# A hybrid attention and gating layer on eight cores: where its attention pieces stand among the full matrix products, and a closing norm in halves

## The reference

```python
h = rmsnorm(x, norm_g)
proj = einsum('bsd,de->bse', h, w_in) + b_in                 # 1024 -> 2816
q, k, v, z_a, u_s, v_s, z_s = split(proj, ...)
# 8 query heads, 2 key/value heads, window of 128, a learned sink per head
attn = banded_sink_attention(q, k, v, sinks) * silu(z_a)
# 8 channel groups, a masked lower-triangular 128x128 matrix each, chunks of 128
sgu = gelu(u_s) * (W_s @ layernorm(gelu(v_s)) + b_s) * silu(z_s)
x = x + concat([attn, sgu]) @ w_out + b_out                  # 1024 -> 1024
out = rmsnorm(x, final_norm_g)
```

## Time and profile before

| | |
|---|---|
| median of 3 runs | 523.46 us (521.31 to 564.06) |
| time of the profiled execution | 525.54 us |
| its span on the slowest core (core 1) | 524.0 us |
| spans of the eight cores | 514.8 to 524.0 us |
| TensorE busy (matmuls) | 498.0 us, 95% of the span |
| ACT, DVE, POOL busy | 63%, 57%, 45% |

### The profile page before, as it was taken

The page is one execution under the profiler, slowest core; times in us unless marked ns, Lnnn a source line. Parts: engine busy times, 40 slices in busy tenths (PEclk is TensorE's granted clock), DMA queues, the critical chain, the costliest instruction groups (busy, mean ns, idle before and its releaser), DMA issues.

```text
span 524.0 us, 10243 instructions; the slowest of 8 cores (514.8 to 524.0 us)
## 1 busy us (share of the span) xinstructions
PE 498.0 (95%) x3443; PEld 238.4 (45%) x3443; DVE 297.7 (57%) x429; ACT 332.0 (63%) x551; POOL 233.3 (45%) x270
## 2 busy tenths in 40 slices
PE   6798889999999999999999999999999999999993
PEld 2356345444454445444454445444454444544441
DVE  3865876564545465454646544554655546666556
ACT  4335768747688386865868476874859467757332
POOL 2101678360546415481374614473254774545213
PEclk9599989999999999999999999999999999999998
DMA  8999994810329422490229613292226303231024
GB/s 241 327 338 335 312 243 67 201 43 1 121 104 228 113 72 90 127 275 2 81 81 230 173 41 118 90 225 92 82 81 177 65 2 117 86 120 41 2 81 201
DMA packets 43876, 71.12 MB, mean 136 GB/s; under 512 B 27536, under 2 KB 27536, under 8 KB 43824
## 3 DMA queue, kind: packets, MB, share of 16 engines
q1 hardware_dynamic: 42480, 68.17, 43.6%
q0 software_dynamic: 1200, 2.25, 2.7%
q10 hardware_dynamic: 144, 0.05, 0.0%
HBM read 49.48 MB, written 16.78 MB: 126 GB/s over the span
## 4 chain that ended last, share of the span: by engine, by line
PE 81%; POOL 5%; ACT 4%; DVE 4%; issue 3%; DMA 2%; POOLq 0%; SPq 0%; ACTq 0%; DVEq 0%
PE pp L533 41%; PE pp L794 19%; PE pp L597 8%; PE pp L721 3%; PE pp L558 3%; PE pp L730 2%; DMA xa<-x 2%; PE pp L678 1%; PE pp L582 1%; POOL xa L778 1%; POOL uT L649 1%; ACT zsT L543 1%; PE pp L643 1%; POOL st_lr L613 1%; ACT junk L470 1%
## 5 line engine op out<-in xcount | busy, mean ns | idle before, releaser
L533 PE MATMUL pp<-xT,w_fm 128*128 128x512 bf16 x1088 | 253.2, 389 | 3.3 <-ACT xT L524 1.3
L533 PEld LDWEIGHTS pp<-xT,w_fm 128*128 128x128 bf16 x1088 | 106.3, 100 | 136.4 <-issue 27.8
L794 PE MATMUL pp<-w_out_bf,mixT 128*128 128x512 bf16 x512 | 118.6, 380 | 0.0
L778 POOL TENSOR_TENSOR xe<-xe,bout_sb 128x1024 f32<-128x1024 f32 x28 | 65.9, 2353 | 20.8 <-DVE xe L808 11.8
L794 PEld LDWEIGHTS pp<-w_out_bf,mixT 128*128 128x128 bf16 x512 | 47.7, 98 | 58.7 <-issue 4.5
L756 POOL TENSOR_TENSOR mixT<-LR,zaT 128x512 bf16<-128x512 f32 x28 | 32.4, 1156 | 58.8 <-DVE LR L752 54.8
L740 ACT ACTIVATE LR<-pp,esink 128x128 f32<-128x128 f32 x128 | 36.5, 369 | 26.0 <-PE pp L730 15.7
L808 DVE SCALAR_TENSOR_TENSOR xe<-xe,st_fr,gf_sb 128x1024 f32<-128x1024 f32 x28 | 35.9, 1284 | 25.7 <-POOL st_fr L806 14.0
L597 PE MATMUL pp<-w_vs,xT 128*128 128x512 bf16 x224 | 49.8, 379 | 0.1
L799 DVE TENSOR_TENSOR xe<-pp,xe 128x512 f32<-128x512 f32 x56 | 38.4, 686 | 19.9 <-PE pp L794 19.5
L543 ACT ACTIVATE zaT<-pp,pack_a_sb 128x512 bf16<-128x512 f32 x32 | 22.0, 688 | 42.3 <-PE pp L533 42.3
(11 more groups left out here) (84 smaller groups left out, 586.7 us busy)
## 6 DMA issues: line engine op xcount, KB each, us to landing
xa<-x SPq DMA_DIRECT2D x32, 512.0 KB, 5.8
xe<-x SPq DMA_DIRECT2D x28, 512.0 KB, 4.1
out<-xe SPq DMA_DIRECT2D x28, 512.0 KB, 2.8
xe<-w_in SPq DMA_DIRECT2D x12, 512.0 KB, 12.1
mixT<-w_in SPq DMA_DIRECT2D x10, 512.0 KB, 14.3
w_out_bf<-w_out POOLq DMA_DIRECT2D x8, 256.0 KB, 11.9
out<-xa SPq DMA_DIRECT2D x4, 512.0 KB, 2.7
LR<-sgu_wT SPq DMA_DIRECT2D x1, 512.0 KB, 16.1
```

Of the source, the lines that this page charges most:

```text
L533: ins = e.matmul(bank(h), lhsT=w_fm[:, FM.index(cb), k, :], rhs=xT[:, xb, k, :], start=(k == 0), stop=(k == 7))
L778: fn = lambda e: e.tensor_tensor(out=r[:, s, :], in0=r[:, s, :], in1=bout[:], op=ALU.add)
L794: ins = e.matmul(bank(h), lhsT=mixT[:, mb, ec, tt * 128:(tt + 1) * 128], rhs=w_out[:, ec, hf * 512:(hf + 1) * 512], start=(ec == 0), stop= ...
```

## The change

Three things change. First, the planner's input gets an ordering rule: for each stage the full products of its Exp phase are collected (fill), and the S of tile j is held until a given number of them are placed, five per tile in stages 1 to 5, two per tile in stage 6 with its eight tiles, one per tile in stage 0. The pv of tile j-1 is held until the S of tile j is placed. Second, the closing norm of the last stage is rewritten (close_tile): the gain is multiplied in before the statistics are known, into another buffer, and the final scaling is ACT's. Third, for the very last tile the norm goes by halves of 512 values: two sums of squares, the two means joined by a small DVE operation, one half scaled by ACT and one by DVE, two stores of 256 KB on two queues. An unused bank class is dropped.

```diff
+SPREAD = (1, 5, 5, 5, 5, 5, 2)
...
+        fill = {st: [] for st in range(-1, NS)}
+        scores = {st: [] for st in range(NS)}
+        values = {st: [] for st in range(NS)}
...
-            G.op("pe", mm, reads=xkeys(st, range(4)) + [("w", cb)], cost=1.73, alloc=[h], prio=prio, mode="full", gate=ph)
+            o = G.op("pe", mm, reads=xkeys(st, range(4)) + [("w", cb)], cost=1.73, alloc=[h], prio=prio, mode="full", gate=ph)
+            if func is None:
+                fill[st - 1].append(o)
...
+            scores[st - 1 if last else st].append(o)
...
+            values[st - 1 if last else st].append(o)
...
+        def close_tile(n, v0):
+            s = n % 4
+            end = n == NT - 1
+            z, zk = (vs_f[:, 0:2, :].rearrange("p a b -> p (a b)"), [("vs_f", 0), ("vs_f", 1)]) if end else (xe[:, s, :], [("xe", s, 0), ("xe", s, 1)])
+            parts = ((0, 512), (512, 1024)) if end else ((0, 1024),)
+            for i, (a, b) in enumerate(parts):
...
+                G.op("act", lambda e, a=a, b=b, i=i: e.activation(out=junk[:, a:b], in_=xa[:, s, a:b], func=AF.Square, accum_out=st_fe[:, s, i:i + 1]),
...
+                G.op("dve", lambda e, a=a, b=b: e.tensor_tensor(out=z[:, a:b], in0=xa[:, s, a:b], in1=gf[:, a:b], op=ALU.mult),
...
+            G.op("pool", lambda e: e.tensor_scalar(out=st_fm[:, s:s + 1], in0=st_fe[:, s, 0:1], scalar1=1.0 / D, scalar2=EPS,
+                                                   op0=ALU.mult, op1=ALU.add), reads=[("fe", s, 0)], writes=[("fm", s)], cost=0.19, prio=v0)
+            if end:
+                G.op("dve", lambda e: e.scalar_tensor_tensor(out=st_fm[:, s:s + 1], in0=st_fe[:, s, 1:2], scalar=1.0 / D, in1=st_fm[:, s:s + 1],
...
+            G.op("pool", lambda e: e.tensor_tensor(out=st_fr[:, s:s + 1], in0=st_fm[:, s:s + 1], in1=nh[:, 0:1], op=ALU.pow),
...
+                if i == 0:
+                    G.op("act", lambda e, a=a, b=b: e.activation(out=xa[:, s, a:b], in_=z[:, a:b], func=AF.Copy, scale=st_fr[:, s:s + 1]),
...
+                else:
+                    G.op("dve", lambda e, a=a, b=b: e.tensor_scalar(out=xa[:, s, a:b], in0=z[:, a:b], scalar1=st_fr[:, s:s + 1], scalar2=None, op0=ALU.mult),
...
+                G.op(("sp", "act")[end and i == 0], lambda e, a=a, b=b: e.dma_start(out=out_d[n * 128:(n + 1) * 128, a:b], in_=xa[:, s, a:b]),
...
+        for st in range(NS - 1):
+            between = sorted(fill[st], key=lambda o: (o.prio, o.n))
+            for j, o in enumerate(scores[st][1:], 1):
+                o.after += (between[SPREAD[st] * j - 1],)
+                values[st][j - 1].after += (o,)
```

More of the change, by code:

```diff
@@ L109 @@
     ENGS = ("pe", "act", "dve", "pool", "sp")
[L110 to L111 removed]
+    CAPS = {"S": 4, "V": 2, "P": 4}
+    PLACES = {"S": (0,), "V": (4, 6), "P": (6, 7, 5, 4)}
     def __init__(self, graph, warm, warmed):
@@ L560, in mmv @@
                 return ins
-            G.op("pe", mmv, reads=xkeys(st, range(4)) + [("w", CB_V)], cost=1.79, alloc=[h], prio=v0 + 0.3, mode="full")
+            o = G.op("pe", mmv, reads=xkeys(st, range(4)) + [("w", CB_V)], cost=1.79, alloc=[h], prio=v0 + 0.3, mode="full")
+            fill[st - 1].append(o)
             def vsrc(lo, a, b):
@@ L599, in mmvs @@
                     return ins
-                G.op("pe", mmvs, reads=[("xT", xb, tt)] + [("w", CB_VS + c) for c in range(4)], cost=1.73,
+                o = G.op("pe", mmvs, reads=[("xT", xb, tt)] + [("w", CB_VS + c) for c in range(4)], cost=1.73,
                      alloc=[h], prio=v0, mode="full", gate=3 * st - 1)
+                fill[st - 1].append(o)
             G.op("dve", lambda e: e.tensor_tensor(out=vs_f[:, vb, :], in0=bank(h), in1=bvs[:], op=ALU.add), uses=[h],
@@ L687, in mms @@
                 return ins
-            G.op("pe", mms, reads=[("qT", qb, c) for c in range(4)] + [("kT", (n - 1) // 4 % 3), ("kT", n // 4 % 3)], cost=0.45, alloc=[S],
+            o = G.op("pe", mms, reads=[("qT", qb, c) for c in range(4)] + [("kT", (n - 1) // 4 % 3), ("kT", n // 4 % 3)], cost=0.45, alloc=[S],
                  prio=v0 - 10, mode="quad", gate=ph)
+            scores[st - 1 if last else st].append(o)
             if first:
@@ L779, in load_xe @@
             G.op({"pool": (2.35, fn)}, None, reads=["c_bout"], writes=keys, prio=st + 0.4 + 0.1 * s, port=True)
+        def close_tile(n, v0):
[4 more added lines that the diff above has]
+            for i, (a, b) in enumerate(parts):
+                ykeys = [("xh", s, i)] if end else [("xh", s, 0), ("xh", s, 1)]
+                zkeys = [zk[i]] if end else zk
+                G.op("act", lambda e, a=a, b=b, i=i: e.activation(out=junk[:, a:b], in_=xa[:, s, a:b], func=AF.Square, accum_out=st_fe[:, s, i:i + 1]),
+                     reads=ykeys, writes=[("junk", "junk1")[i], ("fe", s, i)], cost=0.38 + 0.87 * (b - a) / 1024, prio=v0 - 0.7)
+                G.op("dve", lambda e, a=a, b=b: e.tensor_tensor(out=z[:, a:b], in0=xa[:, s, a:b], in1=gf[:, a:b], op=ALU.mult),
+                     reads=ykeys + ["c_gf"], writes=zkeys, cost=0.04 + 1.24 * (b - a) / 1024, prio=v0 - 0.2, port=True)
+            G.op("pool", lambda e: e.tensor_scalar(out=st_fm[:, s:s + 1], in0=st_fe[:, s, 0:1], scalar1=1.0 / D, scalar2=EPS,
+                                                   op0=ALU.mult, op1=ALU.add), reads=[("fe", s, 0)], writes=[("fm", s)], cost=0.19, prio=v0)
+            if end:
+                G.op("dve", lambda e: e.scalar_tensor_tensor(out=st_fm[:, s:s + 1], in0=st_fe[:, s, 1:2], scalar=1.0 / D, in1=st_fm[:, s:s + 1],
+                                                             op0=ALU.mult, op1=ALU.add),
+                     reads=[("fe", s, 1)], writes=[("fm", s)], cost=0.1, prio=v0 - 0.8)
+            G.op("pool", lambda e: e.tensor_tensor(out=st_fr[:, s:s + 1], in0=st_fm[:, s:s + 1], in1=nh[:, 0:1], op=ALU.pow),
+                 reads=[("fm", s), "nh"], writes=[("fr", s)], cost=0.57, prio=v0)
+            for i, (a, b) in enumerate(parts):
+                ykeys = [("xh", s, i)] if end else [("xh", s, 0), ("xh", s, 1)]
+                zkeys = [zk[i]] if end else zk
+                if i == 0:
+                    G.op("act", lambda e, a=a, b=b: e.activation(out=xa[:, s, a:b], in_=z[:, a:b], func=AF.Copy, scale=st_fr[:, s:s + 1]),
+                         reads=[("fr", s)] + zkeys, writes=ykeys, cost=0.2 + 0.96 * (b - a) / 1024, prio=v0)
+                else:
+                    G.op("dve", lambda e, a=a, b=b: e.tensor_scalar(out=xa[:, s, a:b], in0=z[:, a:b], scalar1=st_fr[:, s:s + 1], scalar2=None, op0=ALU.mult),
+                         reads=[("fr", s)] + zkeys, writes=ykeys, cost=0.4, prio=v0 - 0.8, port=True)
+                G.op(("sp", "act")[end and i == 0], lambda e, a=a, b=b: e.dma_start(out=out_d[n * 128:(n + 1) * 128, a:b], in_=xa[:, s, a:b]),
+                     reads=ykeys, cost=0.5, dsem=d_fin if end and i == 0 else d_st[s], kb=(b - a) // 2, prio=v0, final=True)
@@ L796, in mmo @@
                     return ins
-                G.op("pe", mmo, reads=[("mixA", mb, tt)] + ([("mixC", c) for c in (1, 2, 3)] if st == NS - 1 else []) + [("mixS", mb, jj) for jj in range(4)] + [("w_out", k) for k in range(8)],
+                o = G.op("pe", mmo, reads=[("mixA", mb, tt)] + ([("mixC", c) for c in (1, 2, 3)] if st == NS - 1 else []) + [("mixS", mb, jj) for jj in range(4)] + [("w_out", k) for k in range(8)],
                      cost=1.73, alloc=[h], prio=v0 + 0.05 * hf, mode="full")
+                if st + 1 < NS:
+                    fill[st + 1].append(o)
                 G.op("dve", lambda e, hf=hf, h=h: e.tensor_tensor(out=r[:, s, hf * 512:(hf + 1) * 512], in0=bank(h),
@@ L801, in out_tile @@
                      uses=[h], reads=rin, writes=[(rk, s, hf)], cost=0.68, prio=v0 - 0.5)
+            if st == NS - 1:
+                close_tile(n, v0)
+                return
             G.op("act", lambda e: e.activation(out=junk[:], in_=r[:, s, :], func=AF.Square, accum_out=st_fs[:, s:s + 1]),
```

6 lines of the change are left out of this document (3 added, 3 removed).

## The result

The changed kernel takes 527.75 us (median of 6 runs, 526.83 to 529.68), the kernel before 523.39 beside it (521.31 to 564.06); the ratio is 1.0089, 95% interval 1.0064 to 1.0113. Forecast were 520.1 us and a range of 515.5 to 524.5: wrong in sign and out of the range. The profiled execution of the kernel before was one in which one die takes over 1% longer at a lower clock, and the ratios leave such executions out, while the medians do not.

The account below looks back on a forecast made before the run. TensorE, busy 498.0 of 524.0 us, was taken to bound the kernel. Spread +0.6, stall -0.6, norm -1.2 and clock -2.2 sum to -3.4 us: from the median of 523.46 to 520.1 us, range 515.5 to 524.5.

Parts of the forecast that it names:

- Bound: Steady stages: TensorE is busy 498.0 of 524.0 us overall, and a better overlap has nothing left to win.
- Excursions, +0.6: TensorE going from full products to S and pv and back: -1.0 to +1.5 us for the spread, taken as +0.6.
- The mixing's 0.4 us stays: its banks are still emptied by ACT at the same rate: TensorE's wait at the mixing, on a bank that ACT empties, would stay as it was, 0.4 us at most.
- With five products per tile each has room: Behind a delayed S: five products take 8.7 us against 1.4 + 1.0 for exp and mask, so each has room.
- Stage 6, -0.6: The first pv's 0.57 us wait for the mask would be hidden by six full products: -0.6 us, at worst 0.
- Clock, -2.2: Stretches at 0.81 clock on one die: two of five steady cuts gone, -2.2 us, bounds 0 and -5.5.
- rival (b): All five steady clock cuts to 0.81 go: 516.8 us; chance 0.20 for 515.5 to 518.5.
- Closing norm, -1.2: At the end, from last add to last scaling, with halves and stores: -1.2 us, between 0 and -1.8.
- store term of +0.2: At the end, the last tile but one's later 512 KB store runs into the last halves: 0 to +0.6 us, taken +0.2.
- the multiplications by the gain lie beside the products: Gain multiplications and ACT's earlier scalings lie beside 3.5 us of products per tile; without that cover 1.3 and 1.1 us.
- (c): Slower: q waits for transposed x in three nine-product stages; 529.8 us at 2.5 us late; chance 0.10 for over 524.
- (d): Full products wait for banks held longer by pv, only the norm gains: 522 us; chance 0.30, shared with no clock gain.

Follow-up runs that it names:

- e1: The changed kernel without the ordering rule: order of attention as before, closing norm in halves; 521.71 us, ratio 1.0026 to the kernel before.
- e3: The changed kernel with DVE's two scalings of x behind the first two operations emptying the mixing's banks in stages 3 and 5; 523.85 us, ratio 1.0073.
- e7: The kernel before with the ordering rule for stage 6 alone and the old closing norm; 521.38 us, ratio 1.0011.
- e12: The kernel before with the first pv of stage 6 held until the fifth product of its phase is placed; 520.53 us, ratio 1.0007.
- later measurement: The changed kernel timed again without any edit, beside the kernel before; ratio 1.0107 (1.0075 to 1.0140).
- e13: e9b without the store of the last tile but one, so 128 rows of the output are not written; 519.58 us, ratio 0.9973.
- e9b: e1 with the gain of stage 7 read from PSUM; 520.82 us, ratio 0.9995 to the kernel before.
- e6: e3 with the ordering rule left out for stage 0; 525.7 us, ratio 1.0086 to the kernel before.
- e14: e3 with the gain of the last stage read from PSUM; 524.88 us, ratio 1.0085 to the kernel before.

## Why the prediction was wrong

**Bound.** That the stages have nothing left to win by overlap was not contradicted: stages 1 to 5 are alike on all cores of `e1`, each within 0.1 us, and no other order here makes the five shorter in sum. That cut the other way: where there is so little to win, a new order has mostly losses to bring.

**Excursions, +0.6: right as a price.** The pair is 1.44 (13 of the 14 on core 2), between the ends of 1.32 and 1.50; 7 x 1.32 + 11 x 1.53 + 14 x 1.44 = 46.2 against 45.6.

**"The mixing's 0.4 us stays: its banks are still emptied by ACT at the same rate": the step that failed.** The mixing's own wait stayed. But with it the spread's sum put every other wait for a bank at nothing, and the four banks that the mixing fills are emptied by DVE. What stands in DVE's queue there was not read: the planner, given a new order on TensorE, also moved the scalings of x, two of them from ACT to DVE. That is 2 us in each of stages 3 and 5, of which `e3` gives back some 1.4, and 1.7 us more where 1.2 GHz follows. The forecast priced a new order on one engine with the other engines' queues left as they were, though the planner fixes all of them ahead of the run.

**"With five products per tile each has room": failed too.** It holds between S and pv of one tile. The last pv of a stage stands close behind the one before, and V has one pair of banks: 0.35 us in the row at 154.24, of the 0.4 to 0.5 that stages 1 and 4 lose. Stage 0, whose mixing the rule sets in a row, costs 1.3 to 1.6 us on cores 1 and 2; the forecast had no term for it.

**Stage 6, -0.6: right in sign, -1.3 measured**, though not to be had alone (`e7`, `e12`). On the core of the earlier trace rows, where pv waited 0.57 us, the stage took 66.34 us; on core 2 of `e1`, where it waits 1.0, 67.13. Against the first the gain is 0.5, about what was forecast, against the second 1.3; what else made the first stage shorter is not known.

**Clock, -2.2: not a matter of the order alone, and its size stays open.** In the earlier trace rows the clock was read as a property of the order. But 0.81 stands only in the two traces of the first measurement, on die 0 of both; `e1`, with the order of before, has none on any core, so there was none to win back there. The other die, which showed none in the same trace, said so. In the first measurement the five steady stretches did go, as rival (b) had it; by the lengths of the stages on cores 1 and 6 of the trace of before they were worth 4.8 us, not 5.5. No other trace of the kernel before was taken there, so what such stretches cost in the times compared is not known. The ratio there (1.0089) is lower by 0.9 us than in the later measurement (1.0107), and the intervals overlap: a gain of the clock is neither shown nor excluded. The Trainium skill (TensorE: Matmul & The Clock Gate, Part 1) has the limit held while dense matmuls last on a die's cores. The traces differ: they show it for 4.5 to 7.5 us at a time, and the same products at 1.00 around it.

**Closing norm, -1.2: mis-sized.** (Its own terms reach from -1.5 to -0.5, not from -1.8 to 0.) The half sum of squares and the halves of the scaling came near their price, 0.8 instead of 1.1 (3.9 us instead of 4.7 from the last add on), and the last add came 0.4 earlier behind its product. Two terms took it back. The store term of +0.2 was +0.8, of which `e13` shows 0.7 to be the store ahead. And "the multiplications by the gain lie beside the products" named TensorE as cover and forgot POOL: in the order of before they make the norm a loss of 1.1 us, which the gain in PSUM takes away (`e9b`). In the changed kernel the end is 0 to 0.2 us shorter.

**Rivals.** (c) pointed at the scalings of x, but looked at q behind their transposes, not at the banks behind them in DVE's queue. (d), products waiting for banks, came nearest, and was priced at nothing lost. Forecast to measured: the spread's +0.6 is 6.9 to 9.2 us in stages 0 to 5 (table, cores 1 and 2), 4.0 to 5.6 of it in stages 3 and 5; -0.6 is -1.3; -1.2 is 0 to -0.2; what became of -2.2 is open. The time over 524, which the forecast gave to (c) with 0.10, came about by another mechanism.

**Open.** What the spread costs beyond stages 0, 3 and 5 is spread over banks, loads and the two-way waits of DVE and POOL, and differs by core; that it moves when one wait is taken away is shown (`e6`, `e14`), what sets it on a given core is not. Loading x for the output earlier, ahead of the phase, was not tried. No version here that writes the whole output beats the kernel before.

## What to carry to other kernels

Where a planner places all engines from one list, a rule that reorders one engine is a new program on all of them: read, for each bank that the moved products share, what stands ahead of the operation that empties it on its engine. Where the dies of one trace differ, a term is taken from the clock of the slower one only if a second trace of the same kernel shows it too. At an end without matmuls, cover by TensorE is worth nothing: ask which engine shares a port or a queue with each step that is added.
